# Two attentions of a transformer's first block: pipeline one unit deeper, four score banks, and the position-bias table added up on GpSimd during the input product

## The reference, cut to what matters

```python
def gqa_attend(q, k, v):                       # layer 0: 6 query heads, 2 key heads
    s = jnp.einsum("bqkgd,bnkd->bkgqn", q, k) * HEAD_DIM ** -0.5
    p = jax.nn.softmax(s, axis=-1)
    return jnp.einsum("bkgqn,bnkd->bqkgd", p, v)

# layer 1, mixer_na: 8 heads of 128, 256 image tokens, 256 context tokens
q, k, v = jnp.split(h_lat @ w_in, 3, axis=-1)
s_loc = jnp.einsum("bqhd,bnhd->bhqn", qi, kb) * scale + bias   # bias = rpb[head, row distance, column distance]
s_loc = jnp.where(mask, s_loc, NEG_INF)
s_ctx = jnp.einsum("bqhd,bnhd->bhqn", qi, kc) * scale
p = jax.nn.softmax(jnp.concatenate([s_loc, s_ctx], axis=-1), axis=-1)
```

## Time and profile before

| | |
|---|---|
| time of three runs | 3449.52, 3459.43, 3460.34 us, median 3459.43 |
| the profiled execution's own time | 3446.41 us |
| its span, first to last instruction | 3444.6 us |
| mean granted TensorE clock | 0.871 of 2.4 GHz |
| TensorE busy | 2594.0 us, 75% of the span |
| VectorE busy | 1201.1 us, 35% |
| ScalarE busy | 827.3 us, 24% |
| GpSimd busy | 240.0 us, 7% |
| DMA, mean over the span | 234 GB/s |
| layer 0's attention, scores of two following wide units (512 keys) start | 186.73 and 189.03 us |
| the same, narrow units (256 keys) | 218.49 and 219.92 us |

### The profile page before, as it was taken

One profiled execution on the slowest core, in us unless ns is written; L12 is line 12 of the kernel. 1 busy time (PEld: TensorE's weight loads), 2 busy tenths in 40 slices (PEclk: granted clock), 3 DMA queues, 4 the chain that ended last, 5 costly groups with the idle time before them and its releaser, 6 DMA issues. The chain is left out here.

```text
span 3444.6 us, 43615 instructions
## 1 busy us (share of the span) xinstructions
PE 2594.0 (75%) x17184; PEld 1794.8 (52%) x17184; DVE 1201.1 (35%) x1759; ACT 827.3 (24%) x1199; POOL 240.0 (7%) x200
## 2 busy tenths in 40 slices
PE   5677389999773298468774532999768989989699
PEld 4556334443221175233221211997545979987598
DVE  2344421111004534231000014537634445445443
ACT  2041001111110122111110002435523344334443
POOL 0000240000004100020000010000000000000000
PEclk8898699999896599789887765999889999999899
DMA  6465538999997621279999974433142435342352
GB/s 246 174 260 209 236 119 331 395 424 425 426 425 273 220 98 68 73 255 410 425 426 426 425 289 175 192 147 129 47 185 98 184 133 208 136 154 98 147 208 79
DMA packets 118808, 807.41 MB, mean 234 GB/s; under 512 B 31336, under 2 KB 32936, under 8 KB 66536
## 3 DMA queue, kind: packets, MB, share of 16 engines
q1 hardware_dynamic: 85976, 718.84, 52.1%
q0 software_dynamic: 18304, 50.51, 4.1%
q10 hardware_dynamic: 14352, 35.66, 2.6%
HBM read 758.71 MB, written 56.84 MB: 237 GB/s over the span
## 5 line engine op out<-in xcount | busy, mean ns | idle before, releaser
L2055 PE MATMUL psum<-second_x_hi,ffn_up_hi 128*128 128x256 f32 x1408 | 402.3, 286 | 45.2 <-DVE ffn_up_lo L2130 45.2
L2055 PE MATMUL psum<-second_x_hi,ffn_up_lo 128*128 128x256 f32 x1408 | 401.6, 285 | 0.0
L2055 PE MATMUL psum<-second_x_lo,ffn_up_hi 128*128 128x256 f32 x1408 | 401.6, 285 | 0.0
L1511 PE MATMUL psum<-experts_ahead_ring_up,moe_cols 128*64 128x512 f32 x1568 | 348.8, 597 | 0.0
L2055 PEld LDWEIGHTS psum<-second_x_hi,ffn_up_hi 128*128 128x128 f32 x1408 | 273.8, 194 | 47.7 <-DVE ffn_up_lo L2130 46.3
L1532 PE MATMUL psum<-experts_ahead_ring_down,experts_ahead_counting 128*64 128x512 f32 x784 | 210.8, 687 | 98.3 <-issue 97.4
L2055 PEld LDWEIGHTS psum<-second_x_lo,ffn_up_hi 128*128 128x128 f32 x1408 | 273.7, 194 | 1.4
L2055 PEld LDWEIGHTS psum<-second_x_hi,ffn_up_lo 128*128 128x128 f32 x1408 | 273.5, 194 | 0.0
L2130 DVE TENSOR_TENSOR ffn_up_lo<-second_ring_up,ffn_up_hi 128x4096 fp32r<-128x4096 f32 x44 | 194.4, 4425 | 120.9 <-ACT ffn_up_hi L2092 120.9
L1511 PEld LDWEIGHTS psum<-experts_ahead_ring_up,moe_cols 128*64 128x64 f32 x1568 | 108.5, 137 | 205.1 <-issue 203.9
L1722 DVE TENSOR_TENSOR experts_gated<-experts_silu,psum 128x256 f32<-128x256 f32 (+1 forms) x87 | 31.6, 363 | 500.9 <-ACT experts_silu L1636 500.9
(11 more groups left out here) (450 smaller groups left out, 4279.2 us busy)
## 6 DMA issues: line engine op xcount, KB each, us to landing
experts_ahead_ring_up<-in_experts SPq DMA_DIRECT2D x130, 2048.0 KB, 23.7
experts_ahead_ring_down<-in_experts SPq DMA_DIRECT2D x130, 1024.0 KB, 24.3
second_ring_up<-in_ffn SPq DMA_DIRECT2D x44, 2048.0 KB, 9.3
second_ring_down<-in_ffn SPq DMA_DIRECT2D x44, 1024.0 KB, 5.0
results<-experts_y ACTq DMA_DIRECT2D x49, 512.0 KB, 10.4
second_ring_up<-in_attn_w_qkv SPq DMA_DIRECT2D x9, 2048.0 KB, 8.8
results<-ab_att_zeros SPq DMA_DIRECT2D x32, 512.0 KB, 13.6
ab_ahead_ab_in_w<-in_w_mod SPq DMA_DIRECT2D x6, 2048.0 KB, 16.9
```

Source lines behind the costliest of these rows:

```text
L1511: last = nc.tensor.matmul(psum[64 * e:64 * e + 64, bank, :], x[:, k, 64 * e:64 * e + 64], w[:, k, :, :].rearrange("p a n -> p (a n)"), sta ...
L2055: last = nc.tensor.matmul(psum[:, 2 * m + kind, 0:LAT], w[:, j, k, at], h[:, k, :], start=k == 0 and which == 0, stop=k == KD - 1 and whic ...
```

## The change

- `attention_stage`: the turning of a unit is done two steps after its scores, the value product three, the output four. Scores rotate over four single banks, turned pieces over two single banks; `probs` has three buffers. ScalarE copies the turned unit s-2 before it exponentiates unit s. Both attentions of the first block use it.
- `bias.finish` runs on GpSimd inside the block of the input product of layer 1 (`on_pool`), no longer on VectorE in its own block.
- The loads of `na_out` and of the three vectors are issued by SyncE inside the attention's block (`loads`), no longer in two blocks of their own.
- A third form of bias entry (`factor`), which neither attention uses, is dropped.
- The change's title also names ranked experts; the diff has no line on experts.

```diff
-def split_product_stage(nc, name, psum, stream, n_tiles, operands, drain, shape):
+def split_product_stage(nc, name, psum, stream, n_tiles, operands, drain, shape, on_pool=None):
+        if on_pool is not None:
+            @block.gpsimd
+            def _(pool):
+                on_pool(pool)
...
-        probs = st.sbuf("probs", [P, 2, widest])
+        probs = st.sbuf("probs", [P, 3, widest])
...
         def scores(u):
-            return psum[:, 2 * (u % 2):2 * (u % 2) + 2, :].rearrange("p b n -> p (b n)")
-        turned_ps = psum[:, 4:6, :].rearrange("p b n -> p (b n)")
+            return psum[:, u % 4, :]
+        def turned_ps(u):
+            return psum[:, 4 + u % 2, :]
...
         @block.tensor
-            for step in range(n + 2):
+            for step in range(n + 3):
-                    if u >= 2:
-                        pe.wait_ge(probs_ready, u - 1)
+                    if u >= 4:
+                        pe.wait_ge(probs_ready, u - 3)
...
-                if 0 <= step - 1 < n:
-                    u = step - 1
-                    pe.wait_ge(probs_ready, u + 1)
-                    if u >= 1:
-                        pe.wait_ge(turned_out, u)
                 if 0 <= step - 2 < n:
                     u = step - 2
+                    pe.wait_ge(probs_ready, u + 1)
+                    if u >= 2:
+                        pe.wait_ge(turned_out, u - 1)
...
+                if 0 <= step - 3 < n:
+                    u = step - 3
                     pe.wait_ge(turned_out, u + 1)
...
         @block.vector
-                if 0 <= step - 2 < n:
-                    u = step - 2
+                if 0 <= step - 4 < n:
+                    u = step - 4
                     dve.wait_ge(outs_ready, u + 1)
...
         @block.scalar
-            for step in range(n + 1):
+            for step in range(n + 2):
+                if 0 <= step - 2 < n:
+                    u = step - 2
+                    act.wait_ge(turned, u + 1)
+                    if u >= 2:
+                        act.wait_ge(outs_ready, u - 1)
+                    nc.scalar.activation(probs_t[:, u % 2, 0:n_keys(units[u])], turned_ps(u)[:, 0:n_keys(units[u])],
+                                         ACT.Copy).then_inc(turned_out, 1)
                 if step < n:
                     u = step
                     act.wait_ge(peak_ready, u + 1)
-                    if u >= 2:
-                        act.wait_ge(turned, u - 1)
+                    if u >= 3:
+                        act.wait_ge(turned, u - 2)
...
-                if step >= 1:
-                    u = step - 1
-                    act.wait_ge(turned, u + 1)
...
-    def finish(self):
+    def finish(self, pool):
-        with nc.Block() as block:
-            @block.vector
-            def _(dve):
-                dve.wait_ge(self.loaded, 16 * (1 + 4 * NA_HEADS))
+        pool.wait_ge(self.loaded, 16 * (1 + 4 * NA_HEADS))
...
-                    nc.vector.tensor_tensor(out, right_to_left, mask[:].unsqueeze(1).to_broadcast([P, NA_HEADS * GRID_ROWS, GRID_W]), ALU.add).then_inc(self.masked, 1)
+            nc.gpsimd.tensor_tensor(out, right_to_left, mask[:].unsqueeze(1).to_broadcast([P, NA_HEADS * GRID_ROWS, GRID_W]), ALU.add).then_inc(self.masked, 1)
...
-                    na_projections(nc, psum, cols, stream, q, k, v)
-                out_stream = WeightStream(nc, st, "na_out", chunk_list(i["na_w_out"]))
-                vectors.start()
-                bias.finish()
+                    na_projections(nc, psum, cols, stream, q, k, v, bias.finish)
+                out_stream = WeightStream(nc, st, "na_out", chunk_list(i["na_w_out"]), starts=False)
+
+                def next_loads(sp):
+                    for c in range(out_stream.depth):
+                        out_stream.load(sp, c)
+                    vectors.loads(sp)
...
-                    lambda u: acc[:, u[1], u[0] * HEAD:(u[0] + 1) * HEAD], HEAD)
+                    lambda u: acc[:, u[1], u[0] * HEAD:(u[0] + 1) * HEAD], HEAD, loads=next_loads)
```

More of the change, by code:

```diff
@@ L552, in _, with loads @@
             def _(sp):
-                for i, v in enumerate(self.vectors):
-                    sp.dma_start(self.buf[:, i, :], rows_of(v)).then_inc(self.loaded[i], 16)
+                self.loads(sp)
+    def loads(self, sp):
+        for i, v in enumerate(self.vectors):
+            sp.dma_start(self.buf[:, i, :], rows_of(v)).then_inc(self.loaded[i], 16)
     def wait(self, eng, i):
@@ L664, in attention_stage @@
         chain_sem = st.sem("chain")
+        if idle_fill is not None:
+            zeros, filled, cleared = st.sbuf("zeros", [P, D]), st.sem("filled"), st.sem("cleared")
         block = st.block()
         if idle_fill is not None:
-            zeros, filled, cleared = st.sbuf("zeros", [P, D]), st.sem("filled"), st.sem("cleared")
             @block.gpsimd
@@ L728, in _ @@
             chain = Chain(dve, chain_sem)
-            for step in range(n + 2):
+            for step in range(n + 4):
                 if step < n:
@@ L736, in _ @@
                             dve.wait_ge(probs_ready, u - 1)
-                        for at, table, factor in bias(units[u]):
+                        for at, table in bias(units[u]):
                             if table is None:
                                 ins = nc.vector.tensor_scalar(biased[:, u % 2, at], scores(u)[:, at], scale, None, ALU.mult)
-                            elif factor is None:
+                            else:
                                 ins = nc.vector.scalar_tensor_tensor(biased[:, u % 2, at], scores(u)[:, at], scale, table, ALU.mult, ALU.add)
-                            else:
-                                ins = nc.vector.scalar_tensor_tensor(biased[:, u % 2, at], table, factor, scores(u)[:, at], ALU.mult, ALU.add)
                         chain.then(ins)
@@ L2215, in drain @@
         return copy_on(nc, engine, v[:, t, (c - 4) * BANK:(c - 3) * BANK], bank)
-    split_product_stage(nc, "na_in", psum, stream, lambda c: 4, operands, drain, lambda c, t: (P, LAT if c < 2 else TOK))
+    split_product_stage(nc, "na_in", psum, stream, lambda c: 4, operands, drain, lambda c, t: (P, LAT if c < 2 else TOK), on_pool)
 def split_rows_product(nc, name, psum, cols, stream, tok_tiles, dst):
```

48 lines of the change are left out of this document (24 added, 24 removed).

## The result

The changed kernel took 3433.26 us (median of seven runs, 3428.82 to 3439.09), the kernel before 3449.52 (seven runs, 3443.98 to 3464.43). The medians differ by 16.3 us. The ratio is 0.9946, 95% interval 0.9931 to 0.9960: 18.6 us less, 14 to 24. In a second comparison, on one chip with the last experiment, it was 0.9951 (0.9938 to 0.9964), 16.9 us. The forecast was a gain of 16.5 us. Its time, 3442.9, is 9.6 too high because it was counted from the median of the first three runs of before, 3459.4; seven runs put that median at 3449.5.

A forecast was written before the change was run, and what follows sets the result against it. Bounds: waiting in a closed chain over three engines in layer 1's attention, stores of zeros in layer 0's. Terms 7.9 + 11.0 - 2.7 + 0.3 = 16.5 us off 3459.4 gave 3442.9; range 3429 to 3456.

The forecast's parts named there:

- The gap: Between layer 1's product and attention: three blocks vanish, loads hidden by the attention at no cost; gain 7.9 us.
- Layer 1's attention: Its stage: pace falls from 2.77 to 2.25 us per unit, length from 49.9 to 38.9; gain 11.0 us.
- the closed chain: Layer 1's attention: loop over three engines, 5.5 us, passing in two periods before and three after, 1.8 us each.
- The additions on GpSimd: Start of layer 1's input product: GpSimd's addition locks out VectorE's `lo`, first matmul later; loss 2.7 us.
- B: Layer 1's product start: GpSimd's additions cost more, both ahead or slower; total gain 11.8 or 13.2 us; chance 0.15.
- C: Layer 1's product start: GpSimd and VectorE do not exclude each other; total gain 19.2 us; chance 0.13 together with Rival E.
- D: Layer 1's product start: slow GpSimd additions on reversed rows starve `lo`; at 20 us each, a loss of 13.6; chance 0.04.
- Layer 0's attention: Its stage: stores of zeros still end it at about 227.0, whatever its own chain gains; gain 0.3 us.
- Rival E: Layer 0's attention: zeros done earlier, so its shortening is real, 5 us more at most; chance 0.13 together with C.
- Rival A: Layer 1's attention: pace stays, only the restored clock shows, about 1.8 us; total gain 7.3, 3452.1 us; chance 0.10.
- the 23.0: Lower end of the range: summed bounds of the terms, 11.6 + 7.9 + 3.5, taken with half the runs' spread.

The follow-up runs named there:

- the last experiment: Changed kernel plus both repairs (GpSimd's additions behind the 6th and 7th `lo`, 8 of 32 zero stores beside `ab_out`), repeated: 3424.95 us, ratio 0.9931.
- the two experiments: Against the changed kernel: new attention only, loads and table in their old blocks, ratio 0.9972; old attention order with table and loads moved, ratio 0.9986.

## Why the prediction was right, point by point

The forecast gain was 16.5 us and the edited stages gave 15.9. The misses partly cancel: the attention gained 0.7 more than forecast, and the other three terms together came out 1.3 worse, of which 0.9 is chance of this pair of traces, as the ledger shows.

1. *The gap.* Forecast 7.9, measured 7.83. The loads in the attention's block cost nothing that shows: the pace is 2.19 us beside them and after them. Taken apart: blocks 3.0, table with its block 4.8.
2. *Layer 1's attention.* Forecast 11.0, measured 11.7 (first score to last output 38.2 against 38.9 forecast and 49.9 before); twelve periods of 2.19 instead of 2.25 make the 0.7. That the attention's new code sets the pace is shown by the old order holding its 2.78 with everything else changed, and the new order reaching 2.2 with the old gap. That it did so because the closed chain now passes in three periods is argued from rows 5: no run takes the deeper order, the four banks and ScalarE's earlier copy apart. The clock was put at about 1.8 us of the gain; the two experiments give 1.6 and 2.05. The pace, 2.19, is TensorE's, which the sum of its three parts gave as 2.2. VectorE's 2.2 was 0.17 too high: I added up whole instructions, but the reciprocal starts 0.07 us after the start of the negation, which lasts 0.15, and the next unit's bias 0.27 after the start of the output, which lasts 0.35.
3. *The additions on GpSimd.* Forecast a loss of 2.7, measured 3.1 in this pair of traces and 2.7 on the average of all: 2.45 until the first matmul, in every trace with the additions there, since one takes 4.5 and not 4.7; and 0.66 behind it. The first piece took 1220.95 - 1212.73 = 8.2 us instead of 7.6, with no wait for the second `lo`, which ended at 1219.2. Its matmuls start 0.21 us apart at half clock, later 0.12; that change came 3.2 us after the first matmul before, and 4.7 after it in the changed kernel, but 3.4 to 5.7 in the six other traces with the same start and 5.1 in the experiment with the attention alone, which has nothing on GpSimd there. So the 0.66 is mostly the chance of when the clock rises. Moving the additions brought the first matmul back to 4.29 us after the block's start. The Trainium skill ("SBUF — State Buffer", section "SBUF: two separate sides") has the rule that of a VectorE instruction with two SBUF inputs and a GpSimd instruction that reads SBUF the one that starts first keeps the other out to its end. The trace agrees in both directions: `lo` waited for the first addition, and the second addition waited 2.06 us for `lo`. Rivals B, C and D fell.
4. *Layer 0's attention.* Forecast a gain of 0.3, measured none: 50.0 us against 49.5, within the spread of the traces. The mechanism stands, the stores end the stage. The 0.3 had been read off the end of the DMA engines' activity (227.0); in the changed kernel it ends in the stretch to 227.5, and the next transfer is at 228.74, past the forecast 227.7 to 228. Rival E fell in this kernel; its estimate of up to 5 us was low for the engines, which finished 6.4 earlier. That the time is to be had was shown by putting eight stores elsewhere: 7.1 us.

Rival A (the pace stays) fell with the first trace.

The ends of the range do not follow from the terms given for them: 3459.4 - 23.0 - 5.4 is 3431 and not 3429, rival A's 3452.1 + 5.4 is 3457.5 and not 3456, and the 3.5 in the 23.0 is the bound of no term. The measured 3433.3 lies inside either way, but near the lower end, because the median of before was too high.

## What to carry to other kernels

A stage that ends in a barrier is as long as its slowest queue: ask of a stage that "runs well" which queue's wait ends last before making its engines faster. In a software pipeline over several engines, add up one engine's work per unit and compare it with the period; where no engine is full, divide the closed chain by the number of units that it may span, and one more buffer and one more step can be enough. The additions on GpSimd were hidden only where VectorE had no `lo`, with its two SBUF inputs, due: place such work behind a semaphore of VectorE's and not at the block's start (116.7 us against 119.8).

## What the runs showed of the hardware

- GpSimd's addition with a repeated mask row and reversed reading costs no more than a plain one: 4.52 to 4.54 us for 2048 columns, 2.2 ns a column, against 2.34 us for 1024, 2.3 ns a column.
- GpSimd and VectorE alternated at the start of layer 1's product, where both had two instructions queued, in all seven traces with the additions there: neither got two in a row.
- At the start of layer 1's product TensorE resumed at half clock in all twelve traces, and its matmuls became shorter 3.2 to 5.7 us after the first one, with no clear order among the kernels.
- An idle TensorE can lose its clock after it has resumed. After 1.37 us of idling six score matmuls took 2.81 us; after 4.36 us, 4.51, with the granted clock at 1.00 during the idle stretch and 0.63 in the one after; after 9.26 us, 5.46. The 4.36 us gap thus cost a further 1.2 us behind it.
